# Expert rows fetched and turned one block at a time in a two-layer encoder with grouped top-2 experts

## The reference

```
idx, wts = route(ht, w_router, router_bias)      # top 2 experts inside the best group of 4
y = moe(ht, idx, wts, moe_w_gu[i], moe_w_dn[i])
x = x + g2[:, None, :] * y.reshape(B, S, D)
...
def expert_block(args):
    xb, e = args
    g, u = jnp.split(xb @ w_gu[e], 2, axis=-1)   # 1024 x 1024
    return (jax.nn.silu(g) * u) @ w_dn[e]        # 512 x 1024
```

## Time and profile before

| what | value |
|---|---|
| median of 3 runs | 1685.73 us (1685.37 to 1686.23) |
| the profiled execution | 1688.84 us, its span 1687.1 us |
| granted TensorE clock, mean | 0.968 of full |
| PE busy | 1545.1 us (92%) |
| DVE busy | 974.3 us (58%) |
| ACT busy | 348.7 us (21%) |
| POOL busy | 175.4 us (10%) |
| moved by DMA | 500.96 MB, mean 297 GB/s |

### The profile page before, as it was taken

The page is one execution under the profiler, slowest core; times in us unless marked ns, Lnnn a source line. Parts: engine busy times, 40 slices in busy tenths (PEclk is TensorE's granted clock), DMA queues, the critical chain, the costliest instruction groups (busy, mean ns, idle before and its releaser), DMA issues.

```text
span 1687.1 us, 40379 instructions
## 1 busy us (share of the span) xinstructions
PE 1545.1 (92%) x17779; PEld 892.8 (53%) x17779; DVE 974.3 (58%) x1632; ACT 348.7 (21%) x708; POOL 175.4 (10%) x212
## 2 busy tenths in 40 slices
PE   3999999989998879899998999897999789999997
PEld 2644555445565546566655444343566455566664
DVE  5677777666555435455554388756565344455555
ACT  3346555131100000010002145613100000000100
POOL 1001211000101000010000122200010000100100
PEclk9999999989999889999999999998999999999999
DMA  9654232499999989989995122056899999988996
GB/s 365 246 215 154 96 109 79 165 345 393 384 401 402 407 352 383 409 318 399 408 427 204 50 75 75 25 225 273 317 401 386 405 404 409 395 328 361 401 426 257
DMA packets 59959, 500.96 MB, mean 297 GB/s; under 512 B 9557, under 2 KB 22290, under 8 KB 43146
## 3 DMA queue, kind: packets, MB, share of 16 engines
q1 hardware_dynamic: 50544, 485.38, 72.7%
q0 software_dynamic: 5088, 7.81, 1.5%
q10 hardware_dynamic: 4154, 5.18, 0.9%
HBM read 497.89 MB, written 6.32 MB: 299 GB/s over the span
## 4 chain that ended last, share of the span: by engine, by line
PE 76%; DMA 12%; DVE 7%; issue 2%; ACT 2%; SPq 1%; PEldq 0%; DVEq 0%; ACTq 0%
PE ps L1155 23%; PE ps L1182 12%; PE ps L1162 11%; PE ps L1047 6%; DMA ring_gu<-in_moe_w_gu_dram 4%; DMA arena<-in_moe_w_gu_dram 4%; DMA ring_gu<-in_w_ada_dram 4%; PE ps L1080 3%; PE ps L964 3%; PE ps L1066 2%; PE ps L1104 2%; PE ps L874 2%; PE ps L984 2%; PE ps L938 2%; PE ps L854 2%
## 5 line engine op out<-in xcount | busy, mean ns | idle before, releaser
L2303 DVE TENSOR_TENSOR x_tok<-x_tok,ps 128x1024 f32<-128x1024 f32 x240 | 282.5, 1217 | 107.8 <-PE ps L1182 107.2
L1155 PE MATMUL ps<-ring_gu,arena 128*32 128x256 f32 x5248 | 311.6, 387 | 35.1 <-DMA ring_gu<-in_moe_w_gu_dram 20.3
L1155 PEld LDWEIGHTS ps<-ring_gu,arena 128*32 128x32 f32 x5248 | 171.3, 112 | 152.3 <-issue 28.9
L2095 DVE TENSOR_TENSOR arena<-arena,ps 128x128 f32<-128x128 f32 x120 | 34.4, 287 | 342.0 <-ACT arena L1622 341.9
L1622 ACT ACTIVATE arena<-ps 128x128 f32<-128x128 f32 x120 | 33.2, 277 | 888.2 <-PE ps L1155 888.2
L1182 PE MATMUL ps<-arena 32*128 32x256 f32 x2880 | 194.6, 384 | 4.2 <-DVE arena L2312 3.0
L714 POOL DMA_INDIRECT arena<-xn_dram,tok_idx x104 | 94.3, 907 | 935.6 <-PE ps L1146 599.1
L1162 PE MATMUL ps<-ring_dn,arena 128*32 128x256 f32 x2624 | 158.7, 383 | 4.6 <-DVE arena L2100 2.5
L1182 PEld LDWEIGHTS ps<-arena 32*128 32x128 f32 x2880 | 142.6, 185 | 37.5 <-issue 25.2
L1155 PE MATMUL ps<-arena 128*32 128x256 f32 x2432 | 143.4, 388 | 18.1 <-DMA arena<-in_moe_w_gu_dram 14.9
L1155 PEld LDWEIGHTS ps<-arena 128*32 128x32 f32 x2432 | 79.1, 112 | 74.3 <-DMA arena<-in_moe_w_gu_dram 15.9
(11 more groups left out here) (355 smaller groups left out, 1737.8 us busy)
## 6 DMA issues: line engine op xcount, KB each, us to landing
ring_gu<-in_moe_w_gu_dram SPq DMA_DIRECT2D x44, 4096.0 KB, 19.0
ring_dn<-in_moe_w_dn_dram SPq DMA_DIRECT2D x43, 2048.0 KB, 17.1
arena<-in_moe_w_gu_dram SPq DMA_DIRECT2D x18, 4096.0 KB, 26.6
arena<-in_moe_w_dn_dram SPq DMA_DIRECT2D x20, 2048.0 KB, 19.9
ring_gu<-in_w_ada_dram SPq DMA_DIRECT2D x12, 2048.0 KB, 20.4
ring_gu<-in_w_ada_dram SPq DMA_DIRECT2D x48, 512.0 KB, 4.9
arena<-in_rnn_w_in_dram SPq DMA_DIRECT2D x8, 1024.0 KB, 7.2
arena<-in_moe_w_gu_dram SPq DMA_DIRECT2D x3, 2048.0 KB, 19.6
```

Source lines behind the costliest of these rows:

```text
L1155: last = mm(ps[s_ * ROWS:(s_ + 1) * ROWS, pb, 0:2 * QF].rearrange("p (a b) -> p a b", a=2), rows[:, k, :], pair[:, :, s_, :], start=(k == ...
L2095: v.tensor_tensor(hmid[:, n % 2, :], hsil[:, n % 2, :], ps[:, gu_bank(n), QF:2 * QF], ALU.mult).then_inc(S["hmid_ready"], 1)
L2303: return v.tensor_tensor(by_quarter, by_quarter, ps[:, bank0:bank0 + TILES, cols * QD:(cols + 1) * QD], ALU.add)
```

## The change

Rows are handled block by block. POOL issues one indirect DMA per block that takes each token as four quarters of 1 KB and writes 128 partitions of 256 elements (`xn_quarters`, the index is 4 x token + quarter, by `pquart`). DVE turns a block with one transpose of 32 x 32 squares (`rows_turned`), from SBUF or, for the picked blocks, straight from PSUM. ACT scales the eight chunks of 32 columns in place (`rows_scaled`); for blocks 0 and 1 DVE takes half of them. `xg` and `xgT` hold four blocks. The picking of the first eight blocks is done one block at a time (`pick`, sixteen matmuls each in four column groups, banks 0 and 1 in turn). The 120 PE transposes of a layer are gone. Banks 0 and 1 then serve odd blocks from block 5 on, so that gate-and-up and down products have two banks each, and their waits on the block before become waits on the one before that. In a step the down product of the block before comes ahead of the placing.

```diff
+NPICK = 2 * FIXED
...
-        xg = view(arena, 12288, D)
-        xgT = view(arena, 14336, 2, KT, P)
+        xg = view(arena, 12288, 4, QD)
+        xgT = view(arena, 14336, 4, KT, ROWS)
         yo = view(arena, 16384, 4, QD)
         hsil = view(arena, 17408, 2, QF)
         hmid = view(arena, 17664, 2, QF)
         hmidT = view(arena, 17920, 2, P)
         tok_f = view(mla_big, TT * NE, NCOL)
-        tok_hot = [view(arena, 13312, SEQ), view(arena, 13824, SEQ), gate_bc[:, 1, HALF:D], view(arena, 18176, SEQ)]
-        more_yo = view(arena, 18688, QD)
-        more_hot = gate_bc[:, 0, 0:HALF]
+        tok_hot = [view(arena, 13312, SEQ), view(arena, 13824, SEQ), gate_bc[:, 1, HALF:D], view(arena, 15360, SEQ)]
+        more_hot = view(arena, 15872, SEQ)
+        more_yo = view(arena, 18176, QD)
+        more_xg = view(arena, 18432, QD)
+        more_xgT = view(arena, 18688, KT, ROWS)
...
+        xn_quarters = xn_dram.rearrange("t (s d) -> (t s) d", s=TILES)
+
         def gu_bank(n):
-            return 5 if n < EARLY and n % 2 else 2
+            return (5 if n < EARLY else 0) if n % 2 else 2
 
         def dn_bank(n):
-            return 6 if n < EARLY and n % 2 else 3
+            return (6 if n < EARLY else 1) if n % 2 else 3
...
-                def gather(t):
-                    pool.wait_ge(S["xT_made"], NU * l + (1 if t == 2 else t))
-                    for q in range(TILES):
-                        col = column(*BLOCKS[TILES * t + q])
-                        part = slice(q * ROWS, (q + 1) * ROWS)
-                        g.indirect_dma_start(xg[part, :], None, xn_dram,
-                                             bass.IndirectOffsetOnAxis(ap=tok_idx[0:ROWS, col:col + 1], axis=0),
-                                             bounds_check=SEQ - 1, oob_is_err=False).then_inc(S["gathered"], 16)
-
-                for t in range(2, MORE_UNIT + 2):
-                    gather(t)
+                def gather(n):
+                    col = column(*BLOCKS[n])
+                    if n < NPICK + 4:
+                        pool.wait_ge(S["picked"], NPICK * (l + 1))
+                    else:
+                        pool.wait_ge(S["rows_turned"], NB * l + n - 3)
+                    g.indirect_dma_start(xg[:, n % 4, :], None, xn_quarters,
+                                         bass.IndirectOffsetOnAxis(ap=tok_idx[:, col:col + 1], axis=0),
+                                         bounds_check=TILES * SEQ - 1, oob_is_err=False).then_inc(S[f"gathered{n % 4}"], 16)
+
+                for n in range(NPICK, MORE_BLOCK + 1):
+                    gather(n)
...
-                def pick_rows(t, hf):
-
-                    g = picked_bank(l, t, hf)
-                    pe.wait_ge(*emptied(before_in_bank(g)))
+                base = NB * l
+
+                def pick(b):
+                    e, half = divmod(b, 2)
+                    if b >= 2:
+                        pe.wait_ge(S["rows_turned"], base + b - 1)
                     for i in range(TT):
-                        pe.wait_ge(S["picks_ready"], 2 * TT * l + TT * t + i + 1)
-                        last = mm(bank(g), picked_hot[t][:, i, :], x_tok[:, i, hf * HALF:(hf + 1) * HALF],
-                                  start=(i == 0), stop=(i == TT - 1))
-                    last.then_inc(S["unit"], 1)
-
-                def picks_transposed(t):
-                    for hf in range(2):
-                        pe.wait_ge(*emptied(picked_bank(l, t, hf)))
-                    if t:
-                        pe.wait_ge(S["xT_a"], NU * l + t)
-                        pe.wait_ge(S["xT_d"], NU * l + t)
-                    for k in range(KT):
-                        last = tr(ps[:, k // 4, (k % 4) * P:(k % 4 + 1) * P], picked_rows[t][:, chunk(1, k)], ident[:, :])
-                    last.then_inc(S["xT_made"], 1)
-
-                for hf in range(2):
-                    pick_rows(0, hf)
+                        pe.wait_ge(S["picks_ready"], TT * (FIXED * l + e) + i + 1)
+                        hot = picked_hot[e // 2][:, i, (e % 2 * 2 + half) * ROWS:(e % 2 * 2 + half + 1) * ROWS]
+                        for s_ in range(TILES):
+                            last = mm(ps[s_ * ROWS:(s_ + 1) * ROWS, b % 2, 0:QD], hot, x_tok[:, i, s_ * QD:(s_ + 1) * QD],
+                                      start=(i == 0), stop=(i == TT - 1))
+                    last.then_inc(S["picked"], 1)
+
                 for n in range(2):
                     pe.wait_ge(*emptied(STAGES[f"logits{l}_{n}"]))
-                picks_transposed(0)
-                pick_rows(1, 0)
+                pick(0)
+                pick(1)
...
-                    if n >= EARLY:
-                        pe.wait_ge(S["yo_ready"], base + n)
-                    elif base + n >= 2:
+                    if base + n >= 2:
                         pe.wait_ge(S["yo_ready"], base + n - 1)
+                    if n == TILES + 1:
+                        pe.wait_ge(S["rows_turned"], base + NPICK)
...
+                    if n in (1, 2, 3):
+                        pick(n + 1)
+                    pe.wait_ge(S["xT_a"], base + n + 1)
+                    if n < 2:
+                        pe.wait_ge(S["xT_d"], 2 * l + n + 1)
                     if n == NB - 1:
                         combine(NPAIR - 2, 0)
                         block_down(n - 1)
                         combine(NPAIR - 2, 1)
                     if j == 0:
                         pe.wait_ge(S[f"gu_in{place % RING}"], gu_landed(place, l))
-                    if n >= EARLY:
-                        pe.wait_ge(S["hmid_ready"], base + n)
-                    elif base + n >= 2:
+                    if base + n >= 2:
                         pe.wait_ge(S["hmid_ready"], base + n - 1)
-                    mine_rows = xgT[:, t % 2, :, q * ROWS:(q + 1) * ROWS]
-                    gate_up(gu_bank(n), mine_rows, GU[place % RING], range(KT // 2))
-                    if q == TILES - 2 and t and t + 1 < NU:
-                        rows_transposed(t + 1)
-                    gate_up(gu_bank(n), mine_rows, GU[place % RING], range(KT // 2, KT)).then_inc(S["gu_done"], 1)
+                    if n == TILES + 1:
+                        pe.wait_ge(S["rows_turned"], base + NPICK - 1)
+                    gate_up(gu_bank(n), xgT[:, n % 4, :, :], GU[place % RING], range(KT)).then_inc(S["gu_done"], 1)
                     if n == TILES - 1:
+                        for b in range(TILES + 1, NPICK):
+                            pick(b)
                         slots_products()
-                        pick_rows(1, 1)
                     if n == TILES:
-                        pe.wait_ge(*emptied(picked_bank(l, 1, 1)))
                         pe.wait_ge(*emptied(STAGES[f"slots{l}"]))
                         pe.wait_ge(S["yo_ready"], base + TILES)
+                    if not block_first(n):
+                        block_down(n - 1)
                     for p, half in COMBINED.get(n, []):
                         combine(p, half)
-                    if not block_first(n):
-                        block_down(n - 1)
                 block_down(NB - 1)
...
-                def rows_out(t):
-                    act.wait_ge(S["xT_made"], NU * l + t + 1)
-                    if t >= 2:
-                        act.wait_ge(S["gu_done"], base + TILES * (t - 1))
-                    for k in range(4):
-                        last = A(xgT[:, t % 2, k, :], ps[:, 0, k * P:(k + 1) * P], ACT.Identity,
+                def rows_scaled(n):
+                    act.wait_ge(S["rows_turned"], base + n + 1)
+                    for k in range(KT // 2 if n < 2 else KT):
+                        last = A(xgT[:, n % 4, k, :], xgT[:, n % 4, k, :], ACT.Identity,
                                  scale=scale_col[:, u, k:k + 1], bias=shift_col[:, u, k:k + 1])
                     last.then_inc(S["xT_a"], 1)
 
-                def picks_out(t, hf):
-                    g = picked_bank(l, t, hf)
-                    act.wait_ge(S["unit"], g + 1)
-                    A(picked_rows[t][:, hf * HALF:(hf + 1) * HALF], bank(g), ACT.Copy).then_inc(S["a_free"], 1)
-
-                act.wait_ge(S["xn_saved1"], 16 * (l + 1))
-                picks_out(0, 0)
-                act.wait_ge(S["xn_saved2"], 16 * (l + 1))
-                rows_out(0)
-                picks_out(1, 0)
+                rows_scaled(0)
+                rows_scaled(1)
...
                     A(hsil[:, n % 2, :], ps[:, gu_bank(n), 0:QF], ACT.Silu).then_inc(S["sil_ready"], 1)
+                    if n + 2 < NB:
+                        rows_scaled(n + 2)
...
+                def rows_turned(n):
+                    if n >= 4:
+                        dve.wait_ge(S["gu_done"], base + n - 3)
+                    if n < NPICK:
+                        dve.wait_ge(S["picked"], NPICK * l + n + 1)
+                        src = ps[:, n % 2, 0:QD]
+                    else:
```

(23 more changed lines are left out.)

105 lines of the change are left out of this document (32 added, 73 removed).

## The result

The changed kernel takes **1642.84 us** (median of 4 runs, 1639.98 to 1647.42) against 1685.98 us for the kernel before beside it: a ratio of 0.9744, 95% interval 0.9715 to 0.9773, 43 us less. The forecast was 1656 with a range of 1640 to 1698: the direction is right, the gain is half as large again as forecast (43 for 30), and it lies near the low end.

The account below looks back on a forecast made before the run. PE was taken to set the pace, with the weight stream's limit close behind. PE's 15.6 us a layer, 31 in all, less 1 for late fetches, gave 30 us off: median 1656 us, range 1640 to 1698.

Parts of the forecast that it names:

- PE, the steps: Expert steps of each layer: eight transposes gone in 13 units at 1.23 us, 16.0 us a layer; DVE and ACT work hidden.
- PE decides: Expert steps: cheaper fetches free 18 to 27 us of stream a layer, more than PE's 15.6, so PE decides; chance 0.55.
- PE's sum: Both layers: 16.0 + 1.5 - 1.9 = 15.6 us a layer, 31 us in all, if the weight stream can follow.
- The stream and the fetches: Weight stream in the expert parts: a group of four fetches costs 0.9 to 1.6 us in the new form instead of 3.0.
- The estimate from the same page's "Bandwidth / Measured": Fetches: 128 KB about 1.3 us by a straight line, 5.3 us a group, making the stream 30 us a layer longer.
- The start: First picks to block 4: 8.9 + 6.3 - 11.2 - 2.3 = 1.7, taken as 1.5 us a layer gained, bounds 4 and -2.
- The end: Block 59: two placings follow each other, the second's wait of 1.49 us grows by 1.86; -1.9 us a layer.
- Two banks each: Expert steps: two banks each and the down product ahead of the placing cost and give nothing, PE having no bank wait.
- The stream decides: Rival, weight stream: the fetch costs the same 3.0 us, only a third of PE's 31 is won, 1676; chance 0.17.
- the fetch costs more: Rival, weight stream: part of the cost goes by rows, now four times as many; 4.2 us a group gives 1707; chance 0.16.
- Late fetches: Rival, expert steps: fetches arrive late, holding DVE's turn and then PE; half of PE's gain lost, 1671; chance 0.12.
- The 0.87 us a packet: Weight queue: packet time per engine; giving way after each, a fetch takes 9 x 0.87 = 7.8 us, over a 7.25 us step.

Follow-up runs that it names:

- experiment 7: Changed kernel with eight idle PE transposes put back ahead of the product in one block of four, 13 times a layer: 1656.16 us, 0.9811.
- experiment 4: Changed kernel with each block fetched a second time, unread, in the old form (32 rows of 4 KB to 32 partitions): 1687.65 us, 0.9997.
- Experiment 6: Kernel before with each block fetched by four DMAs of 32 rows of 1 KB, still to 32 partitions: 1748.62 us, 1.0366.
- experiment 2: Changed kernel with the PSUM bank turns put back by four from layer 1's mixer on, as in the kernel before: 1652.1 us, 0.9799.
- experiment 10: Changed kernel with a layer's last step reordered: down product of block 58, half placing, gate-and-up of block 59, second half placing: 1636.67 us, 0.9691.
- experiment 9: Changed kernel with one bank for gate-and-up and one for down products from block 4 on, each waiting for the block before: 1652.35 us, 0.9799.
- experiment 5: Changed kernel with each block's quarters fetched a second time, unread, in the new form to 128 partitions: 1661.86 us, 0.9854.
- experiment 3: Kernel before, transposes kept, quarters fetched to 128 partitions, values wrong, only layer 0 compared: its steps 457.0 us for 467.8; whole run 1664.94 us.

## Why the prediction was right, and where not

*PE, the steps.* The work taken out is right: 7.26 us in all four blocks, turn 0.65 us and hidden, ACT hidden at 2.5 us for 2.2. What the 16.0 us a layer are worth is not: put back, they cost 5 to 10 us a layer (experiment 7). The step that failed is the sentence by which PE decides once the stream is freed. With the fetches cheap the stream is still at 0.98 of its share:

```profile
400.00:880.00 480.00, 446.55 (x7648) 278.58 (x7636) 273.09 (x477) 155.06 (x514) 52.12 (x52) 0.97 0.98 407
```

against 0.97 in the earlier trace rows, at 407 GB/s for 389. PE and the stream bound the steps together: of 21.1 us in layer 0, the form of the fetch alone brings 10.8. I had counted the fetches' effect as a support of PE's sum and left it out of it ("I count none of it in the sum"). So two terms were mis-sized, in opposite directions: 32 us for the transposes, worth 11 to 19, and nothing for the fetches, worth about 20. That the forecast came as near as it did is in part luck, for these two errors offset each other.

*The stream and the fetches.* The price of the new form, 0.9 to 1.6 us a group, measured 1.3; the old form's 3.0 comes out somewhat lower by the 3.3 times of experiment 4, 3.3 x 0.32 MB at 427 GB/s = 2.5 us. Experiment 6 rules out the length of the row as the reason. Its result fits the reason given, the spread over partitions, but doesn't show it, since the number of rows in a DMA changed with it. The Trainium skill, "DMA: Bandwidth & Descriptors", section "The descriptor swizzle", has each engine write a port of its own in a transfer over 128 partitions. Weight packets of 0.79 us beside a 32-partition fetch and 0.63 without one don't contradict it, but no trace shows a port. The estimate from the same page's "Bandwidth / Measured", 5.3 us a group (5.2 when worked out again), is not what this case measured, 1.3: the table gives a time for each DMA, and the four fetches here pass beside a full stream.

*The start.* Forecast 1.5 us, measured 0 in both layers. The first half was right and better than forecast: the first gate-and-up product comes 5.3 us after the first pick, for 15.2 before. The second half was short: 40.4 us from there to block 4 for 30.4, 10.0 more where the sum had 7.2. Waits of 0.37 and 2.43 us make 2.8 for the 2.3 taken, and the rest is in products that I had not priced again. The slots products take 4.98 us for 3.33. The granted clock is 1.00 there; DVE makes their 0/1 matrices, one pair every 0.69 us, only just ahead of them, and PE waits for these up to the last pair (14 short waits on `L2206` in the two layers, 5.8 us with those of the weight loads). In the kernel before there is no such wait. The two down products behind the wait take 5.05 for 3.66, at a granted clock of 0.71. In experiment 2 the clock stayed at 1.00 behind the same wait, and they took 3.66, so that part comes and goes between executions.

```profile
417.89 2.25 PE L1118 MATMUL ps<-arena 128*128 128x226 f32 x8
420.51 2.73 PE L1118 MATMUL ps<-arena 128*128 128x226 f32 x8 [0.37 <-DVE arena L2206]
425.66 5.05 PE L1139 MATMUL ps<-ring_dn,arena 128*32 128x256 f32 x64 [2.43 <-DVE arena L2054]
```

*The end.* Forecast -1.9 us. The wait grew by that much, 1.49 in the earlier trace rows is 3.35 now, but the half placing behind it takes 3.63 us for 2.01, at a granted clock of 0.53:

```profile
865.50 3.63 PE L1159 MATMUL ps<-arena 32*128 32x256 f32 x32 [3.35 <-DVE arena L2283]
```

So the end costs **3.3 to 3.5 us a layer** (27.7 and 27.6 for 24.2 by the stretch of experiment 10), nearly twice the forecast. The step that failed is that a wait was priced at its own length and not at what the products behind it lose to the clock.

*Two banks each.* Costed at nothing. In the steps that is so, but at blocks 22 and 23 two banks keep off 3 to 5 us a layer (experiment 9) which the new order would have brought. I had looked at the steady step alone.

*Not seen at all:* the 8 to 9 us of the bank turns in layer 1's mixer. The diff says it, in three deleted lines of a list with four entries, and nothing in the view of the expert part could. Without them the gain is 34 us (experiment 2), near the 30 of the forecast.

*Rivals.* "The stream decides", as it was put (the fetch costs the same 3.0 us), and "the fetch costs more" fall with the price of 1.3 us. A part of "the fetch costs more" rested on four times the rows; q0 has no more packets now than before (576 and 582 in 100 us). "Late fetches" is not there: no wait of DVE's turn for a fetch stands in the trace. It is there in experiment 6, with 16 DMAs a unit. The 0.87 us a packet on which that rival was worked out is a mean over sizes: the trace has weight packets of 16 KB in 0.62 us and of 32 KB in 1.2.

By parts then, of 43 us: bank turns 8 to 9; the fetch form 20 to 26 (10.8 in layer 0 with layer 1 taken as the same, or the 26 us between experiments 4 and 5); PE's transposes 11 to 19 (experiment 7); the end of the layers -7; the start 0. That adds up to between 32 and 47 us. The bounds are wide because PE and the stream share one limit and the executions of a kernel scatter, and no run shows the split more closely.

## What to carry to other kernels

Where two resources are both near their limit, price an edit on each of them, and don't take the sum of one as the gain: about half of this gain came from what the fetches stopped doing to the weight stream. Price a new wait of PE with the clock that the products behind it get. Price a DMA by what the other queue moves less beside it, in a stretch that is full, never by its own share. And where an allocation goes by a running count (banks, buffers, slots), an entry added or removed moves everything behind it, even in layers that the change never mentions: compare the waits of the whole program.

## What the hardware showed that I had not expected

- A fetch of 32 rows to 32 partitions takes 3.3 to 4.0 times its own size from a full weight stream, in rows of 4 KB and of 1 KB alike (experiments 4 and 6); one of 128 rows to 128 partitions takes 1.1 to 1.6 times (experiments 5 and 3). Before and after, the cost appears as slower packets of the other queue at an unchanged share (38.60 and 40.27 MB at 95.7 and 95.9%).
- ACT takes 401 ns for 128 x 32 elements with scale and shift by column, 317 ns each in a row of eight, more than the 278 ns of its silu on the four times larger 128 x 128.
- One wait of 5.2 us on PE cost 8 to 9 us, since the products behind it went at a granted clock of 0.93 and took 3.0 us more. One of 3.35 us in place of 1.49 cost 3.5 us more, and not 1.9, with a placing at 0.53 behind it.
